# Input projection of a two-block model: filter sums formed ahead of the magnitudes, norm and first tap's correction half a unit later

## The reference

```python
u = _centred_conv3(h @ w_in + b_in, conv_w, conv_b)      # 1024 x 3072
v, x1, x2 = jnp.split(u, 3, -1)
kf = _hyena_filters(L, f_w1, f_b1, f_freq, f_w2, f_b2, f_w3)
# in _hyena_filters, a is the 64-wide output of a small MLP over positions
h = (a @ f_w3.astype(F32)).reshape(L, 2, HY_ORDER, D_MODEL)
h = h * window[:, None, None, :]
two_sided = jnp.concatenate([h[:, 0], zeros, h[:0:-1, 1]], 0)
two_sided = two_sided / jnp.sum(jnp.abs(two_sided), 0, keepdims=True)
```

## Time and profile before

| | |
|---|---|
| Median of 3 runs | 4597.77 us (4597.29 to 4599.33) |
| Span of the profiled execution | 4598.3 us |
| Mean granted TensorE clock over the span | 0.927 |
| TensorE matmuls busy | 3891.5 us (85% of the span) |
| VectorE busy | 1611.1 us (35%) |
| ScalarE busy | 703.6 us (15%) |
| Projection matmuls, L430 | 768 instructions, 353.0 us busy |

### The profile page before, as it was taken

The page is one execution under the profiler, slowest core; times in us unless marked ns, Lnnn a source line. Parts: engine busy times, 40 slices in busy tenths (PEclk is TensorE's granted clock), DMA queues, the critical chain, the costliest instruction groups (busy, mean ns, idle before and its releaser), DMA issues. The chain is left out here.

```text
span 4598.3 us, 52872 instructions
## 1 busy us (share of the span) xinstructions
PE 3891.5 (85%) x22090; PEld 2180.1 (47%) x22090; DVE 1611.1 (35%) x2672; ACT 703.6 (15%) x1405; POOL 464.9 (10%) x513
## 2 busy tenths in 40 slices
PE   4889989978569999999999946999568996857994
PEld 2333468864224444444444413554447886323442
DVE  4544359974530000000000033440555665252003
ACT  1000012211101001000000012121252332011110
POOL 0000000002000000000000020000205655000110
PEclk8999999999779999999999978999779998878997
DMA  6555422315068888888888832211110000308994
GB/s 247 187 199 188 176 110 102 127 53 195 28 225 310 306 301 310 301 304 310 298 307 309 293 123 94 77 59 57 62 69 3 4 4 36 124 23 306 319 319 156
DMA packets 277056, 807.07 MB, mean 176 GB/s; under 512 B 9697, under 2 KB 16921, under 8 KB 261494
## 3 DMA queue, kind: packets, MB, share of 16 engines
q1 hardware_dynamic: 257722, 715.56, 42.1%
q0 software_dynamic: 18016, 77.89, 5.1%
q10 hardware_dynamic: 1116, 10.71, 0.6%
HBM read 709.46 MB, written 94.66 MB: 175 GB/s over the span
## 5 line engine op out<-in xcount | busy, mean ns | idle before, releaser
L1211 PE MATMUL banks<-moe_ring,moe_xeT 128*128 128x512 f32 x2560 | 1122.6, 595 | 4.4 <-ACT moe_xeT L1265 4.4
L1211 PEld LDWEIGHTS banks<-moe_ring,moe_xeT 128*128 128x128 f32 x2560 | 484.5, 191 | 596.8 <-issue 596.8
L1231 PE MATMUL banks<-moe_ring,moe_hidT 128*128 128x512 f32 x1280 | 565.7, 595 | 21.6 <-ACT moe_hidT L1272 21.6
L1301 DVE TENSOR_TENSOR moe_hid<-moe_silu,banks 128x512 f32<-128x512 f32 x80 | 55.0, 687 | 1295.3 <-PE banks L1211 1295.3
L1231 PEld LDWEIGHTS banks<-moe_ring,moe_hidT 128*128 128x128 f32 x1280 | 240.6, 190 | 320.0 <-issue 290.8
L1497 PE MATMUL banks<-hT,w_in_ring 128*128 128x512 f32 (+3 forms) x976 | 364.2, 536 | 4.3 <-ACT hT L1520 4.3
L430 PE MATMUL banks<-hT,w_in_ring 128*128 128x512 f32 x768 | 353.0, 615 | 3.9 <-ACT hT L452 3.9
L1497 PEld LDWEIGHTS banks<-hT,w_in_ring 128*128 128x128 f32 (+1 forms) x976 | 183.5, 188 | 184.7 <-issue 172.4
L961 PE MATMUL banks<-w_out,mix 128*128 128x512 f32 x512 | 231.4, 610 | 12.5 <-DMA w_out<-d_w_out 11.3
L430 PEld LDWEIGHTS banks<-hT,w_in_ring 128*128 128x128 f32 x768 | 147.7, 197 | 195.9 <-issue 186.1
L1280 ACT ACTIVATE moe_silu<-banks 128x512 f32<-128x512 f32 x80 | 47.8, 597 | 1204.7 <-PE banks L1211 1204.7
(11 more groups left out here) (408 smaller groups left out, 4214.2 us busy)
## 6 DMA issues: line engine op xcount, KB each, us to landing
moe_ring<-d_wg SPq DMA_DIRECT2D x80, 2048.0 KB, 12.7
moe_ring<-d_wu SPq DMA_DIRECT2D x80, 2048.0 KB, 17.5
moe_ring<-d_wd SPq DMA_DIRECT2D x80, 2048.0 KB, 8.0
x_normed<-d_ada_w SPq DMA_DIRECT2D x12, 2048.0 KB, 8.1
x_normed<-d_mod_w SPq DMA_DIRECT2D x8, 2048.0 KB, 8.3
d_taps<-dft SPq DMA_DIRECT2D x8, 2048.0 KB, 7.3
taps_in<-d_taps SPq DMA_DIRECT2D x8, 2048.0 KB, 10.0
w_in_ring<-d_hy_w_in SPq DMA_DIRECT2D x6, 2048.0 KB, 8.9
```

Source lines behind the costliest of these rows:

```text
L1211: last = nc.tensor.matmul(m.ps[:, 2 * kind + c, :], xeT[:, k, :], up(c, kind)[:, k, :], start=(k == 0), stop=(k == KT - 1))
L1231: last = nc.tensor.matmul(m.ps[:, Y_BANK + h, :], hidT[:, c, i * P:(i + 1) * P], down(c)[:, i, h * BANK:(h + 1) * BANK], start=(fc == 0 an ...
L1301: nc.vector.tensor_tensor(hid[:, j % 2, :], sg[:, j % 2, :], m.ps[:, 2 + j % 2, :], ALU.mult).then_inc(s.hid, 1)
```

## The change

On VectorE, `sum_diff` of the next turn moves from behind the magnitudes to a place ahead of the odd unit's convolution, right behind the unit's windowed products. The second `windowed` of a unit moves ahead of `direct`. On TensorE, `norms` moves from behind the first half's filter pair to behind the second half's. No instruction is added or removed.

```diff
-                    if h == 0 and 2 <= unit <= 2 * N_IT and unit % 2 == 0:
+                    if h == 1 and 2 <= unit <= 2 * N_IT and unit % 2 == 0:
                         norms(unit // 2 - 1)
...
                 if unit < 2 * N_IT:
                     windowed(2 * unit)
+                    windowed(2 * unit + 1)
+                if unit % 2 == 1 and unit // 2 + 1 < N_IT:
+                    sum_diff(unit // 2 + 1)
                 if 2 <= unit <= 2 * N_IT and unit % 2 == 0:
                     direct(unit // 2 - 1, gen)
-                if unit < 2 * N_IT:
-                    windowed(2 * unit + 1)
                 if unit == 2 * N_IT:
                     scaled_taps(gen)
...
                 if unit % 2 == 1 and unit < 2 * N_IT:
                     magnitudes(unit // 2, gen)
-                    if unit // 2 + 1 < N_IT:
-                        sum_diff(unit // 2 + 1)
```

## The result

The changed kernel takes 4536.32 us (median of 4 runs, 4534.77 to 4537.84); the kernel before, run beside it, 4598.55 us (4 runs, 4597.29 to 4609.33). The ratio is 0.9862, 95% interval 0.985 to 0.9874: 62 us less. The forecast was 4536.7.

What follows compares the result with a forecast made beforehand. TensorE plus its stops, with the clock falling behind them, was taken to bound the projection stage. 40.3 us of waits and 20.8 of slow work, 61.1 together, off 4598.3 gave 4537.2, less half a us 4536.7; range 4528 to 4553.

Steps and rivals of the forecast that it cites:

- The stops and their cause: Input projection: TensorE's filter matmuls wait 35.5 us for sum and difference behind VectorE's reductions; the norm waits 4.8 us.
- The sum: Even units 2 to 16 shrink from 223.15 to 162.0 us, a gain of 61.1 us.
- slow work: Projection stage's TensorE work running at 1.2 GHz behind the stops; 20.8 us of the forecast gain.
- the norm's bounds: Norm on TensorE in even units takes 0.9 to 1.82 us, giving a gain of 62.7 to 55.4 us.
- the 6 us: Allowance both ways for later stages, whose stops have a clock recovery that depends on the moment.
- The thin place: Even unit's second filter pair waits for VectorE's windowed product behind the magnitudes; met with 1.3 us to spare.
- The correction later: First tap's two VectorE operations wait for the later norm; hidden by 15 us before the next reader, costed at nothing.
- SyncE's queue: Store moves to about 18.7 us into the unit; weights land within 14.5 us at worst, 3 us left; about 260 GB/s.
- The rival in which it still falls: Even units' clock still falls in the small work behind the second filter pair; only 40.3 us gained, 4557.5; chance 0.05.
- The slower rival: Weights land too late for VectorE's moved sum in odd units, stopping TensorE; 4612 us at 36 us landing; chance 0.02.
- the point of no effect: TensorE is touched only when the moved sum comes later than 47 us from the even unit's start.

Runs made afterwards that it cites:

- The added quarter: Changed kernel plus one further VectorE reduction over a quarter of the row in the magnitudes, each of eight turns: 4533.90 us.
- the doubled reductions: Three kernels: changed kernel with the magnitudes' second reduction, first reduction, or both run twice: 4556.50, 4568.26 and 4610.20 us.
- The late loads: Changed kernel with weights, window and bias loads of turns 2 to 7 issued at the end of the odd unit ahead of their turn: 4587.66 us.

## Why the prediction was right

*The stops and their cause.* Right. The earlier trace rows name the waits, VectorE's order in the earlier trace rows explains them, and the two single moves show that each, made alone, leaves a stop in units 2 to 14: 32.0 us at the norm or 35.4 at the filter pair.

*The sum.* Forecast 61.1 us out of 223.15 − 162.0, measured 62.16 out of 223.15 − 160.99. The 1 us is the norm: in units 2 to 14 it adds 20.45 − 19.50 = 0.95 us, where I took 1.1 out of 0.9 to 1.82. In unit 16 it adds 17.89 − 16.73 = 1.16. Of the 62.16 us, 40.23 were idle and 21.9 slow work, against 40.3 and 20.8 forecast. The norm's speed at 2.4 GHz, said to stand in no row, could in part have been read: in unit 16 of the kernel before one of the two L413 matmuls took 377 ns, as all 16 do in the changed kernel (377 to 378).

*From the stage to the end.* The spans differ by 62.5 us. Before unit 2 the new execution lost 1.3 us (unit 2 starts at 126.03, not 124.72), all of it in the stage's very first half (see the last section), and from the stage's last transposes on it is 1.7 us shorter: 4598.3 − 604.17 = 3994.1 before, 4535.8 − 543.33 = 3992.5 after. 62.16 − 1.3 + 1.7 = 62.5. I had allowed 6 us for this. I took the span for the profiled execution's time, while in the new execution 1.7 us lie around it; the forecast does not hang on that, since it comes to the median before less 61.1.

*The luck.* The gain between the medians was 4598.55 − 4536.32 = 62.2 us, 1.1 more than forecast, and the kernel before came out 0.8 us higher than the 4597.77 from which the forecast started. The two nearly cancel, and the runs of one kernel scatter by 3 us and more, so meeting the median within 0.4 us is luck; the gain within 1.1 us is what the working earns. The bounds given beside the forecast, 4530 to 4546, are not quite the sum of their terms either: the norm's bounds and the 6 us together give 4529 to 4548.

*The thin place.* 1.3 us of slack forecast, 1.5 measured in unit 4; the sum and the difference push the rest by 0.68 us, not 0.8, as VectorE's instructions overlap a little (the convolution, L567, starts 1.88 us behind L505, where it was 1.20). The added quarter confirms it from one side, the doubled reductions from the other.

*The correction later.* Costed at nothing; without its new place the time is 4536.17. Right.

*SyncE's queue.* Store 18.7 us into the unit, landing at most 14.4 us: as forecast. The mean rate of units 3 and 4 is (350 x 19.50 + 192 x 20.45) / 39.95 = 269 GB/s, near the 260 that I worked out from the same two units before; over units 2 and 3 it is 236.

*The clock.* The rival in which it still falls is out: 1.00 in every even unit, with norm, transposes and modulation matmuls in a row. The Trainium skill ("TensorE: Matmul & The Clock Gate", section "A second HAM failure mode: psum-queue depth-cycling") tells of a kernel that changes PSUM banks in each iteration, whose small gaps between groups of matmuls made the clock swing. The trace of this loop does not show it: it changes banks too, and from 126.03 to 426.28 us TensorE is busy throughout at 1.00.

*The slower rival was worked out wrongly.* It was said to touch TensorE from a sum 47 us into the pair of units, and to turn the change slower from a landing of about 34 us. The late loads show another point. There unit 2 begins at 125.62 and L494 comes at 172.60, 47.0 us later, where I had set the point of no effect; the stops behind it were 0.7 and 6.4 us. The step that was left out is VectorE's work behind the waiting sum. The count has to start at the windowed product's slack: 1.5 us late is free (2.4 in units 6, 10 and 14), everything beyond it costs the second filter pair. Even so that kernel is 12 us faster than the one before. Its stretch is 349.52 − 300.25 = 49.3 us longer over six turns; some 2 us more per turn would use up the 62 us. That puts the landing from which the change turns slower at about 29 us, not 34; this is an estimate from these figures, no run went there.

## What to carry to other kernels

When one engine's two waits hang on the same work of another engine, moving either alone only shows the other (4.3 and 1.1 us in units 2 to 14 here), and both together give far more (54 us): look behind each wait for the next instruction that needs the same work. An in-order engine should form what the next turn needs before it does the long work of this turn, if the inputs are there. Price a stop on TensorE with the slow work that follows it, from rows of the kernel at hand: 21.9 us on 40.2 here.

## What the runs showed of the hardware that I had not expected

The slow work behind a stop of one length is not one number: behind 5.4 us it was 1.4 to 4.0 us, behind 6.7 us 1.3 or 4.2 us, behind 2.3 us nothing or 3.2 us. So a stop's length alone does not set its price. What does beside it, such as the moment at which the stop falls, was not tested.

The stage's very first half, the same matmuls, took 7.13 us in three of the ten profiled executions, 8.83 in the kernel before and 10.11 in the changed one. The granted clock from 87.1 to 94.1 us was 1.00, 0.76 and 0.57 there, so up to 3 us lie between executions at one place. The idle time ahead of it (3.4 to 3.5, 3.89 and 3.16 us) does not order them; what does was not looked into.

VectorE's second reduction takes longer in the changed kernel, as its row shows (ns, min/median/max):

```profile
L518 DVE TENSOR_REDUCE h_sums<-h_larger x8: 3660/3668/3673, 135.0 to 416.7; 128x256 f32<-128x2048 f32 x8
```

It took 3591 to 3599 ns in the earlier trace rows, when TensorE stood still beside it. In the kernel with late loads it was 3.59 us at 183.24, inside a stop of TensorE, and 3.62 at 229.07, where the stop covered only its last 2.1 us. That it is TensorE's running that costs the 0.07 us fits these rows and was not tested.
